# Layer norm after the expert stages: row statistics moved to ScalarE, ln_g and ln_b spread on the chip from one row

## The reference

```python
def layer_norm(x, g, b):
    mu = jnp.mean(xf, axis=-1, keepdims=True)
    var = jnp.mean(jnp.square(xf - mu), axis=-1, keepdims=True)
    return ((xf - mu) * lax.rsqrt(var + LN_EPS) * g + b).astype(x.dtype)
...
for layer in range(DEPTH):
    ...                                                      # mixer: hp
    xp = layer_norm(alpha * xp + hp, ln_g[layer, 0], ln_b[layer, 0])
    xp = layer_norm(alpha * xp + hier_moe(xp, *moe_w), ln_g[layer, 1], ln_b[layer, 1])
```

## Time and profile before

| | |
|---|---|
| median of three runs | 1508.51 us (1505.11 to 1510.57) |
| the profiled execution | 1509.92 us, its span 1508.2 us |
| mean granted TensorE clock | 0.91 |
| busy, share of span: PE, DVE, ACT, POOL | 85%, 22%, 16%, 8% |
| chain that ended last: PE, DMA, SP queue, issue, DVE | 41%, 36%, 7%, 7%, 4% |
| bytes moved by DMA | 476.36 MB, mean 316 GB/s |

### The profile page before, as it was taken

How to read it: one execution, slowest core, us unless ns; L and a number is a source line. 1 busy time by engine, 2 the same in 40 slices (tenths; PEclk the granted TensorE clock), 3 DMA queues, 4 the chain that set the end, 5 groups by cost and what they waited for, 6 DMA issues and landing times.

```text
span 1508.2 us, 14792 instructions
## 1 busy us (share of the span) xinstructions
PE 1287.2 (85%) x5744; PEld 585.1 (39%) x5744; DVE 337.5 (22%) x1110; ACT 239.8 (16%) x525; POOL 122.3 (8%) x167
## 2 busy tenths in 40 slices
PE   7999999689988998999873998769988989898880
PEld 5756544433323332333222775433323323333230
DVE  0153325521111111111005222431111111111005
ACT  1123341021111111111110000111111111111110
POOL 3101110100000000010001000100100000001001
PEclk9998799779999999999995999769999999999995
DMA  8840634949999999999989244349999999999972
GB/s 211 216 168 11 172 98 172 416 165 420 418 422 419 421 421 419 422 419 419 421 322 343 86 168 169 138 187 375 421 420 423 420 420 420 420 420 420 419 292 97
DMA packets 95507, 476.36 MB, mean 316 GB/s; under 512 B 16207, under 2 KB 21887, under 8 KB 79052
## 3 DMA queue, kind: packets, MB, share of 16 engines
q1 hardware_dynamic: 83268, 458.73, 75.5%
q0 software_dynamic: 11104, 13.80, 3.5%
q10 hardware_dynamic: 1064, 2.86, 0.6%
HBM read 476.93 MB, written 22.52 MB: 331 GB/s over the span
## 4 chain that ended last, share of the span: by engine, by line
PE 41%; DMA 36%; issue 7%; SPq 7%; DVE 4%; POOL 2%; ACT 1%; POOLq 0%; ACTq 0%; DVEq 0%
DMA mem<-w_exp_up 34%; PE bank L1541 9%; PE bank L1538 7%; SPq L399 7%; PE bank L1654 6%; PE bank L1553 4%; PE bank L1422 4%; PE bank L1234 4%; ACT mem L641 1%; PE bank L1385 1%; PE bank L1492 1%; POOL mem L565 1%; DMA mem<-y_rows 1%; DVE mem L1192 1%; PE bank L1304 1%
## 5 line engine op out<-in xcount | busy, mean ns | idle before, releaser
L1541 PE MATMUL bank<-mem 128*64 128x512 f32 x1024 | 496.4, 642 | 85.7 <-DMA mem<-w_exp_up 85.7
L1538 PE MATMUL bank<-mem 128*64 128x512 f32 x1024 | 506.3, 644 | 4.4 <-ACT mem L641 3.0
L1541 PEld LDWEIGHTS bank<-mem 128*64 128x64 f32 x1024 | 144.9, 147 | 345.0 <-issue 217.6
L641 ACT COPY mem<-bank 64x512 f32<-64x512 f32 (+7 forms) x343 | 165.9, 501 | 590.7 <-PE bank L1234 199.3
L1553 PE MATMUL bank<-mem 128*64 128x512 f32 x1024 | 241.9, 605 | 2.1 <-DVE mem L1164 2.1
L1159 DVE TENSOR_TENSOR mem<-mem,bank 64x512 f32<-64x512 f32 x64 | 44.3, 691 | 610.9 <-ACT mem L644 610.9
L1234 PE MATMUL bank<-mem 128*128 128x128 f32 (+4 forms) x790 | 123.7, 290 | 61.4 <-DVE mem L1031 33.5
L1538 PEld LDWEIGHTS bank<-mem 128*64 128x64 f32 x1024 | 141.0, 146 | 81.8 <-issue 74.0
L1234 PEld LDWEIGHTS bank<-mem 128*128 128x128 f32 (+4 forms) x790 | 88.9, 166 | 158.7 <-issue 104.0
L644 ACT ACTIVATE mem<-bank 64x512 f32<-64x512 f32 x64 | 37.7, 589 | 588.7 <-PE bank L1541 588.7
L1553 PEld LDWEIGHTS bank<-mem 128*64 128x64 f32 x1024 | 70.8, 138 | 121.9 <-issue 115.5
(11 more groups left out here) (174 smaller groups left out, 629.4 us busy)
## 6 DMA issues: line engine op xcount, KB each, us to landing
mem<-w_exp_gate SPq DMA_DIRECT2D x64, 2048.0 KB, 32.8
mem<-w_exp_up SPq DMA_DIRECT2D x64, 2048.0 KB, 31.5
mem<-w_exp_down SPq DMA_DIRECT2D x64, 2048.0 KB, 35.4
mem<-w_conv_in SPq DMA_DIRECT2D x6, 2048.0 KB, 19.4
mem<-w_attn_in SPq DMA_DIRECT2D x5, 2048.0 KB, 16.1
mem<-w_attn_out SPq DMA_DIRECT2D x1, 4096.0 KB, 16.2
mem<-cache_k_a SPq DMA_DIRECT2D x16, 256.0 KB, 2.5
mem<-y_rows SPq DMA_DIRECT2D x8, 512.0 KB, 6.2
```

The lines of the kernel that those rows point to most:

```text
L641: return nc.scalar.copy(out, in_)
L1538: mm(out[0:CAP, :], x[:, c, :], wg[:, c, :], start=c == 0, stop=c == DC - 1)
L1541: last = mm(out[CAP:2 * CAP, :], x[:, c, :], wu[:, c, :], start=c == 0, stop=c == DC - 1)
```

## The change

- **Loading.** For the second normalisation of each layer, `load_ln_rows` takes the place of `load_ln`: `ln_g` and `ln_b` are loaded as one row of 4 KB each, into partitions 64 and 96 of tile 2 of `X`, which has only 32 rows in use. The first normalisation of each layer keeps `load_ln`.
- **Spreading.** At the end of TensorE's expert stage four matmuls of a row of ones (one partition deep) with half a row of 512 columns write `ln_g` and `ln_b` to all partitions of banks 0 to 3; ScalarE copies the four banks to `LNP` and raises `ln_set`.
- **Statistics.** `row_stats` on ScalarE does four activations per tile: a sum of the row (Identity with accumulation), times -1/1024, the sum of squares of x minus mean (Square with that as bias), times 1/1024 plus epsilon. Each waits for the one before. The full-width results go to `YG` and are not read.
- **VectorE** does all six multiply-adds first, and then for each tile the two passes `(x + negative mean) * ln_g` and `x * rstd + ln_b`. The power stays on GpSimd.
- `WORK` grows by 16 columns for three small tiles, and three semaphores are added.

```diff
+    LNR = [X[64 + 32 * p:65 + 32 * p, 2, :] for p in range(2)]
...
+        def load_ln_rows(k):
+            for p, name in enumerate(("ln_g", "ln_b")):
+                sp.dma_start(LNR[p], t[name][k // 2, k % 2].rearrange("(o d) -> o d", o=1)).then_inc(ld_ln, 16)
...
             sp.wait_ge(ln_done, 6 * layer + 3)
-            load_ln(2 * layer + 1)
+            load_ln_rows(2 * layer + 1)
...
# ScalarE, end of experts(layer)
+            act.wait_ge(ln_rows, layer + 1)
+            for p in range(2):
+                for half in range(2):
+                    last = copy(LNP[:, p, 512 * half:512 * half + 512], bank[2 * p + half][:, :])
+            last.then_inc(ln_set, 1)
...
+        def row_stats(layer):
+            for j, i in enumerate(STEPS):
+                n, m = TILES[i][1], 3 * (3 * layer + j)
+                x, junk, col = X[0:n, i, :], YG[0:n, 2 * j, :], slice(i, i + 1)
+                act.wait_ge(y_used, 6 * layer + 2 * j + 2)
+                nc.scalar.activation(junk, x, ACT.Identity, accum_out=LSUM[0:n, col]).then_inc(ln_part, 1)
+                act.wait_ge(ln_part, m + 1)
+                nc.scalar.activation(LMEAN[0:n, col], LSUM[0:n, col], ACT.Copy, scale=-1.0 / D).then_inc(ln_part, 1)
+                act.wait_ge(ln_part, m + 2)
+                nc.scalar.activation(junk, x, ACT.Square, bias=LMEAN[0:n, col], accum_out=LSQ[0:n, col]).then_inc(ln_part, 1)
+                act.wait_ge(ln_part, m + 3)
+                nc.scalar.activation(VE[0:n, col], LSQ[0:n, col], ACT.Copy, scale=1.0 / D, bias=EPS).then_inc(ln_stat, 1)
...
         act.dma_start(SCW[16:19, :], t["conv_w"][0]).then_inc(ld_state, 16)
+        row_stats(0)
         act.wait_ge(cv_in_T, 1)
...
         experts(1)
+        row_stats(1)
...
# VectorE, end of experts(layer), behind the two multiply-adds of each tile
-                norm_rows(2 * layer + 1, j)
+            for j, i in enumerate(STEPS):
+                n, m = TILES[i][1], 3 * (2 * layer + 1) + j + 1
+                x = X[0:n, i, :]
+                if j == 0:
+                    dve.wait_ge(ln_set, layer + 1)
+                dve.wait_ge(ln_stat, m)
+                link(V_.scalar_tensor_tensor(x, x, LMEAN[0:n, i:i + 1], LNP[0:n, 0, :], ALU.add, ALU.mult))
+                dve.wait_ge(ln_rstd, m)
+                V_.scalar_tensor_tensor(x, x, RSTD[0:n, i:i + 1], LNP[0:n, 1, :], ALU.mult, ALU.add).then_inc(ln_done, 1)
...
# TensorE, end of experts(layer)
+            pe.wait_ge(ld_ln, 32 * (2 * layer + 2))
+            for p in range(2):
+                for half in range(2):
+                    last = mm(bank[2 * p + half][:, :], ONE[64 + 32 * p:65 + 32 * p, :], LNR[p][:, 512 * half:512 * half + 512],
+                              start=True, stop=True)
+            last.then_inc(ln_rows, 1)
```

More of the change, by code:

```diff
@@ L140, in build_in @@
     S0 = TOTAL - 3 * SLOT
-    WORK = 9536
+    WORK = 9552
     common = region(0, WORK)
@@ L155, in build_in @@
     STATS, MV, VE, RSTD = common(12), common(3, 2), common(3), common(3)
+    LSUM, LMEAN, LSQ = common(3), common(3), common(3)
     XT_BANKS, LG_BANKS, RK_BANKS = (5, 6), (0, 4, 2), (7, 1, 3)
@@ L249, in build_in @@
         sem("smp_" + n) for n in ("scored", "exp", "p", "T", "Tevac", "O", "cut", "yT", "y"))
-    op_psum, ln_stat, ln_rstd, ln_done = (sem(n) for n in ("op_psum", "ln_stat", "ln_rstd", "ln_done"))
+    op_psum, ln_part, ln_stat, ln_rstd, ln_done = (sem(n) for n in ("op_psum", "ln_part", "ln_stat", "ln_rstd", "ln_done"))
+    ln_rows, ln_set = sem("ln_rows"), sem("ln_set")
     ro_psum, ro_top, ro_exp, ro_hot, ro_rank, ro_slot = (sem("ro_" + n) for n in ("psum", "top", "exp", "hot", "rank", "slot"))
```

## The result

The changed kernel took 1491.67 us (median of three runs, 1491.41 to 1493.62) against 1508.51 (1505.11 to 1510.57): a ratio of 0.9891, 95% interval [0.9868, 0.9913]. This and every later ratio is to the kernel before, timed in the same group of runs. The profiled execution took 1493.62 us, its span 1491.9.

The account below looks back on a forecast made before the run. It took VectorE's work and its wait for GpSimd's power to bound both expert stages' ends. Gaining 5.06 us at each, 10.1 in all, off the profiled 1509.92 gave 1499.8, or 1498.3 us against the median; range 1493 to 1504.

Parts of the forecast that it names:

- What bounds the ends: Ends of both layers' expert stages: after the first multiply-adds' loads, only VectorE and GpSimd's power end a wait; 20.48 us each.
- The loads: Third multiply-add, now right behind the second: its two loads land by 1483.3 and 1483.8, before use at 1484.7; cost nothing.
- the spreading: Four matmuls and copies (2.4 us) before the first multiply-add, on idle engines, ending some 4 us before y_rows is added.
- the conv weights: Behind layer 0's end: third part there by 811.6, convolution starts at 818.05 for 823.11; 6.4 us of slack, gain passes on.
- ScalarE's copies: Layer 0's end: copies of transposed tiles stand behind all statistics; the first tile's about 0.6 us late, the last tile's free.
- A tile's statistics: ScalarE, both ends: four activations and semaphore steps take 3.3 us a tile, bounds 2.9 and 4.2, ready before VectorE needs them.
- The power: GpSimd's one-column power, both ends: needs a turn between two VectorE instructions, costing VectorE 0 to 0.5 us a tile, taken as 0.42.
- The three turns of an end: One wait of VectorE for GpSimd's power per tile, three tiles at each end, 0.42 us each.
- the rival in which the power has no price: Power takes 1.52 us beside VectorE's passes without delaying them: 6.3 us gained an end, 1495.9 us; chance 0.26.
- The end of the span: Behind the kernel's last pass: earlier tiles' stores are over by then, as before; no gain counted there.
- The range: 1493 to 1504 us: from a free power less 2.5 us scatter to only the kernel's end gaining.

Follow-up runs that it names:

- The order alone: Kernel before, with all six multiply-adds ahead of the first tile's statistics, which stay on VectorE: 1508.95 us, ratio 0.9999.
- the statistics alone: Changed kernel with ln_g and ln_b loaded onto all partitions as before, without the matmuls and copies that spread them: 1493.86 us, ratio 0.9904.
- late memset: Changed kernel plus GpSimd setting one unused column behind the last pass, for which nothing waits: 1498.67 us, ratio 0.9947.

## Why the prediction was wrong

- **What bounds the ends** was right: nothing but VectorE's stream and the power, as before's rows had it. The order alone gave nothing, and the stream cut to twelve instructions gave 6.29 us at each end.
- **The loads, the spreading, the conv weights, ScalarE's copies** were right at nothing. The spreading's copies ended later than forecast (1.1 us ahead of the first multiply-add, not 4), which cost nothing. The copies of the transposed tiles were not even 0.6 us late, since a tile's statistics took less than forecast: ScalarE had waited 0.45 us for the first tile's transposes.
- **A tile's statistics** were sized at 3.3 us, with a lower bound of 2.9, and took 2.8: Identity 1.06 and Square 1.15 us to the estimate's 1.15, but a one-column activation 0.20 us and not 0.29, and a semaphore step, for which the forecast had no row, 0.03 to 0.04 and not 0.06. With slack on this engine it moved nothing.
- **The power was the first step that failed.** The step says that the power "needs a turn between two VectorE instructions" and "I take 0.42". Its premise held (alone it takes 0.54 us, and it waits for the running pass), its conclusion did not: who waits is GpSimd alone. The three turns of an end were worth 0; 14.19 us with and without the power, for 15.42 forecast. At two ends that is 2.5 us. The time an end gained, 6.29 us, is that of the rival in which the power has no price, though by another mechanism: the power was not 1.52 us long, it only had to wait. That the rival's number comes out is in part luck: it let the last pass wait for the last power, which in fact ended 2.1 us before that pass began (1484.85 against 1486.97), and the two paths happened to end together in its sum.
- **The end of the span was the second.** The step "The stores of the earlier tiles are over by then, as before" took the stretch behind the last pass as fixed. It fell from 5.6 to 3.6 us. Before, the last power ended at 1501.22, 1.4 us ahead of the last pass's end, and the 7.0 us behind it reached over the store. In the changed kernel the last power ends 3.4 us ahead. The rows of before allowed the question, since 5.6 us is long behind a single store, but one execution of one kernel could not answer it.
- **What is left is scatter.** 1498.3 (its own terms, 1508.51 less twice 5.06, give 1498.4) less 2.5 and 2.0 is 1493.8 us; the changed kernel's later medians are 1494.36 and 1494.62, those of the statistics alone 1493.86. The first median, 1491.67, lies 2 us lower, with runs of the same kernel from 1491.06 to 1498.06. The two later medians lie inside the stated range, so that the first fell below it is in part scatter; the two steps above fail all the same. The stretch from the convolution to the last scatter alone varied from 648.6 to 653.1 us among the profiles, whatever the kernel. Which part of this belongs to the loads in layer 1, where the second multiply-add came 8.4 to 9.5 us behind the scatter, stays open.
- **The range** reached down to the rival with no price less the scatter of the runs. With the 2.0 us that was missing at the span's end it would have reached 1491.4 and not 1493.

## What to carry to other kernels

Take the work off the engine whose stream ends last, and try the order alone to see whether it was the work or the wait: here the order alone gave nothing, and all 12.6 us of the ends came from VectorE's own instructions and its wait for a one-column result. When an operation's duration in the trace depends on what runs beside it, find out which of the two engines waits before charging the other. And look at what each engine does last: one late operation of 0.1 us on GpSimd, for which nobody waited, cost 4.0 us.

## What the runs showed of the hardware that was not expected

- In all 14 profiles the span ends 7.0 us behind GpSimd's last operation (6.98 to 7.05, with a late memset 7.02) or 3.0 us behind the issue of the last store, whichever is later.
- A one-column power on GpSimd takes 0.54 to 0.56 us where VectorE is idle, within 0.05 us of a pass's start, or beside a pass with one input in PSUM. Where it starts 0.15 us or more into a pass with two inputs in SBUF it ends 0.4 us behind that pass, which makes 0.93 to 1.56 us. VectorE is held up by 0.03 us at most, also where the power began first.
- A VectorE pass of 1024 columns takes 1.26 to 1.29 us on 32 rows as on 128; in two halves, one input in PSUM, the pair takes 1.39 to 1.41.
- ScalarE's accumulating activations of 1024 columns take 1.06 (Identity) and 1.15 us (Square), and reading the accumulator 0.19 us, half of it beside the activation's own time.
